# Seven block products in place of eight in two output-and-gate stages, and latent attention in nine stretches

## The chip, the cores and the metric

The kernel runs on 1 core of a Trainium2 chip. The time is device microseconds of one execution of the whole program. Before the change three runs took 4273.81, 4282.54 and 4290.16 us, median 4282.54.

TensorE multiplies (PE; PEld is its weight load), VectorE is DVE, ScalarE is ACT, GpSimd is POOL, SyncE (SP) issues the DMAs. Every matmul result lands in one of 8 PSUM banks of 512 columns; GpSimd cannot read them.

## The reference

Two model blocks one after the other, in float32, on 1024 tokens of width 1024 and 256 context tokens. Block one has a window attention layer and a latent attention layer; block two has a retention and stick-breaking layer and a RWKV-7 layer, each followed by a gated addition. What the change touches is, of block one, the attention of `latent_attention`, and of block two the end of each layer:

```python
def attend(qn, qr, kn, kr, v):                       # 16 heads, 1280 keys, value width 64
    s = (jnp.einsum("bqhd,bkhd->bhqk", qn, kn)       # 64 deep
         + jnp.einsum("bqhd,bkd->bhqk", qr, kr)).astype(F32) * scale   # 32 deep
    p = jax.nn.softmax(s, axis=-1).astype(v.dtype)
    return jnp.einsum("bhqk,bkhd->bqhd", p, v)

for i in range(DEPTH):                               # second block
    ...
    h = h + y                                        # y = mixed @ w_out, 1024 x 1024 by 1024 x 1024
    gate = jax.nn.sigmoid(jnp.einsum('bsd,de->bse', h, ple_gate[i]))
    h = h + gate * jnp.einsum('bsp,pd->bsd', p[i], ple_proj[i])
return rmsnorm(h, final_gain)
```

## The kernel before

All work is cut into row tiles of 128 tokens; there are 8 of them beside 2 of context. The program is a chain of stages with a barrier between them. In each stage every engine has its instructions written out by hand in one order and waits on semaphores (`wait_ge`) that other engines raise (`then_inc`). Nothing is scheduled by a planner.

*Latent attention* (`latent_attention`). The unit of work is a group: one pair of heads (8 pairs) by one pair of row tiles (4 pairs), 32 groups, four 128 x 1280 score blocks each. TensorE makes the scores of the next group in three chunks of 512, 512 and 256 keys into four banks (`scores`, L2107 and L2113). VectorE scales them out of the banks and takes the maxima (`read_scores` L2045, `maxima` L2052 and L2054). ScalarE takes the exponential (`exp` L2011). TensorE turns the result, four 128 x 128 blocks a bank, ten fills a group (`fill` L2122), ScalarE moves each fill to SBUF (`move` L2019), TensorE multiplies by the values (`values` L2134), VectorE copies the product out (`evacuate` L2060), TensorE turns it back (`turn_back` L2141), VectorE divides (`normalise` L2069). Two banks take the fills, one bank per head the outputs. The values of one head are made in two halves, so the TensorE order of a group alternates between scores, fills and values in 14 stretches.

*Output and gate* (`project_and_gate`, called as pg0 after stick-breaking and as pg1 at the end). For each row tile: turn the mixed row, multiply by the output weight (`output`, two halves of 512 columns, 8 blocks of depth each), add to x (L2757), copy x, turn it (L2823), multiply by the gate weight, sigmoid (L2692), multiply by p times its projection (L2763), add to x (L2765). The order interleaves the gate of tile i with the output of tile i + 2, in a loop of six rounds. pg1 also finishes the last row of the RWKV scan (class `LastOutput`; its four passes on GpSimd run from 3995.17 to 4004.34 us), norms each row tile (`norm`, L2707 to L2711 on ScalarE, L2770 on VectorE) and stores it.

*The class `Seven`* stands in the kernel already and serves the latent gate stage (`latent_gate_and_project`). It multiplies two row tiles by a 1024 x 1024 weight as a 2 x 2 block product with seven block multiplications in place of eight. The left operands are sums of blocks s1 to s4, made by GpSimd; the right ones are differences of weight blocks t1 to t4, made by VectorE once per weight; VectorE joins the products (p15, u2, c12, c22, c21). A float32 matmul in the program is two instructions in the trace, so that a block product (4 in depth) shows as x8.

Of the kernel before, what the change touches and what calls it, by code (L numbers as in the profile page):

```python
# [13 lines left out]
P = 128  # L14
# [1135 lines left out]
class Seven:  # L1150


    def __init__(self, nc, mem, name, banks):
# [3 lines left out]
        self.s1, self.s2, self.s3, self.s4 = (sb(f"s{n}", [P, HK, P]) for n in range(1, 5))  # L1157
# [784 lines left out]
def latent_attention(nc, core, q_dram, qr_dram, k_dram, kr_dram, v_dram, o, pair0, prefetch):  # L1942
# [9 lines left out]
    HALVES = [range(0, KT // 2), range(KT // 2, KT)]  # L1952
    unit = lambda h, i: 2 * h + i
    with ExitStack() as mem:
# [7 lines left out]
        pT_moved = [nc.alloc_semaphore(f"{name}_pT_moved{n}") for n in range(2)]  # L1962
# [4 lines left out]
        s_banks, pT_banks, o_banks = [core.banks(n) for n in range(4)], [core.banks(4 + n) for n in range(2)], [core.banks(6 + n) for n in range(2)]  # L1967
# [9 lines left out]
        with nc.Block() as block:  # L1977
# [28 lines left out]
            def _(act):  # L2006
# [7 lines left out]
                def move(g, f):  # L2014
# [4 lines left out]
                    act.activation(pT[:, h, at * BANK:(at + 1) * BANK], pT_banks[f % 2], ACT.Copy).then_inc(pT_moved[f % 2], 1)  # L2019
# [3 lines left out]
                for g in range(G):  # L2023
# [15 lines left out]
            def _(dve):  # L2039
# [32 lines left out]
                for g in range(-1, G + 1):  # L2072
                    if g >= 1:
                        evacuate(g - 1, 0)
                    if g + 1 < G:
                        for j in (0, 2, 1, 3):
                            read_scores(g + 1, 0, j)
                    if g >= 1:
                        normalise(g - 1, 0)
# [3 lines left out]
                    if g >= 1:  # L2083
                        evacuate(g - 1, 1)
# [5 lines left out]
                    if g >= 1:  # L2090
                        normalise(g - 1, 1)

            @block.tensor
            def _(pe):
# [21 lines left out]
                def fill(g, f):  # L2116
                    pe.wait_ge(p_made, 4 * g + (BLOCKS * f + BLOCKS - 1) // KT + 1)
                    if FILLS * g + f >= 2:
                        pe.wait_ge(pT_moved[f % 2], (FILLS * g + f) // 2)
                    for n in range(BLOCKS):  # L2120
                        j, t = (BLOCKS * f + n) // KT, (BLOCKS * f + n) % KT
                        last = pe.transpose(pT_banks[f % 2][:, n * P:(n + 1) * P], s_sb[:, g % 2, j, t * P:(t + 1) * P], core.ident)  # L2122
                    last.then_inc(pT_made, 1)

                def values(g, h, half):
                    if half == 0:
                        for n in range(2):
                            pe.wait_ge(pT_moved[n], (FILLS * g + (h + 1) * FILLS // 2 + 1 - n) // 2)
                        if g:
                            pe.wait_ge(back_read, 2 * (g - 1) + h + 1)  # L2130
# [1827 lines left out]
```

## Time and profile before

The profiled execution took 4284.42 us, its span 4282.6 us, with a mean granted TensorE clock of 0.978. TensorE is busy 4032.9 us (94%), VectorE 1540.1 (36%), ScalarE 1260.7 (29%), GpSimd 408.2 (10%). The DMA queues are busy 16.9% of the time.

| stage | from (us) | to (us) | TensorE busy in a stretch of it |
|---|---|---|---|
| latent attention | 1166 | 1758 | 562.31 of 564 us (1186 to 1750) |
| latent gate (seven products) | 1761 | 1965 | 193.05 of 194 us (1766 to 1960) |
| output and gate, pg0 | 2605 | 2887 | 225.83 of 232 us (2645 to 2877) |
| output and gate, pg1 | 3989 | 4283 | 193.79 of 195 us (4030 to 4225) |

How to read it: an instruction's line is given as L and the line of the kernel, then the engine, the operation, what is written and read, and the count where equal ones are merged. "Idle before" is the time in which the engine waited, and who ended it. Matmuls overlap, so that the time between the starts of two runs is the cost of the first, not its printed length.

### The profile page before, as it was taken

Reading aid. Unit: us, or ns where it says so; the run is one execution under the profiler, and the core shown is the slowest. Engines: PE = TensorE matmul, PEld = TensorE weight load, DVE = VectorE, ACT = ScalarE, POOL = GpSimd, SP = SyncE. Lnnn points to the kernel's source line nnn. Section 1 sums busy time; section 2 is a strip of 40 time slices with the busy share of each in tenths; the row PEclk is TensorE's granted clock in tenths of the full one; section 3 lists DMA queues with packets and bytes.
Section 4 is the critical chain, followed back from the end, with each engine's and each line's share of the span. In section 5 each row is a group of like instructions: output and inputs, shape, how many; then the busy total and the mean of one; then the engine's idle time right before and its main releaser. Section 6 shows DMA issues by size and latency. Waiting matters only on the chain. (4 is left out here: it accounts for less than half of the span.)

```text
span 4282.6 us, 70536 instructions
## 1 busy us (share of the span) xinstructions
PE 4032.9 (94%) x30002; PEld 2372.6 (55%) x30002; DVE 1540.1 (36%) x3355; ACT 1260.7 (29%) x2212; POOL 408.2 (10%) x203
## 2 busy tenths in 40 slices
PE   8999999999899999999999999989999978888998
PEld 3458844445466666544554465444444478787543
DVE  3346621132144444422331063113322356656111
ACT  1147710012255555311220063112222222211233
POOL 0000000000000000331000000000000046655100
PEclk9999999999999999999999999999999999999999
DMA  5000052141410100202012011014111221112200
GB/s 216 20 20 2 2 177 74 35 105 73 154 49 23 46 23 24 89 20 89 15 39 73 12 40 60 0 39 168 49 49 49 84 75 47 62 57 76 101 20 20
DMA packets 166054, 254.28 MB, mean 59 GB/s; under 512 B 49812, under 2 KB 95364, under 8 KB 165766
## 3 DMA queue, kind: packets, MB, share of 16 engines
q1 hardware_dynamic: 165768, 250.09, 16.9%
q8 instruction: 225, 3.69, 0.4%
q14 instruction: 61, 0.50, 0.0%
HBM read 187.76 MB, written 62.05 MB: 58 GB/s over the span
## 5 line engine op out<-in xcount | busy, mean ns | idle before, releaser
L2045 DVE TENSOR_SCALAR_CACHE_REDUCE la_s<-psum 128x512 f32<-128x512 f32 (+1 forms) x384 | 210.5, 598 | 289.7 <-PE psum L2113 289.6
L2019 ACT ACTIVATE la_pT<-psum 128x512 f32<-128x512 f32 x320 | 177.1, 596 | 236.9 <-PE psum L2122 236.9
L286 PE MATMUL psum<-room,pg_oT 128*128 128x512 f32 x512 | 229.0, 606 | 6.5 <-ACT pg_oT L2685 6.5
L286 PE MATMUL psum<-rp_w_last,rp_mixed 128*128 128x512 f32 x512 | 222.2, 592 | 0.0
L2122 PE MATMUL psum<-ident,la_s 128*128 128x128 f32 x1280 | 180.4, 280 | 2.0 <-ACT la_pT L2019 1.9
L2011 ACT ACTIVATE la_s<-la_s,la_negm 128x1280 f32<-128x1280 f32 x128 | 175.2, 1368 | 14.0 <-DVE la_negm L2054 14.0
L1167 POOL TENSOR_TENSOR lg_seven_s<-other_columns 128x512 f32<-128x512 f32 x4 | 5.1, 1267 | 1780.7 <-POOLq L112 1760.2
L286 PE MATMUL psum<-room,columns 128*128 128x512 f32 x400 | 173.3, 592 | 0.0
L286 PEld LDWEIGHTS psum<-room,pg_oT 128*128 128x128 f32 x512 | 99.3, 195 | 131.8 <-issue 127.6
L286 PE MATMUL psum<-room,rp_mixed 128*128 128x512 f32 x384 | 168.2, 594 | 3.0 <-DVE rp_mixed L3087 3.0
L3271 POOL TENSOR_TENSOR room<-room,first_weights 128x1024 f32<-128x1024 f32 x7 | 16.5, 2364 | 1603.6 <-DMA rs_b<-rwkv_raw 1535.1
L2122 PEld LDWEIGHTS psum<-ident,la_s 128*128 128x128 f32 x1280 | 137.9, 140 | 49.0 <-issue 45.3
L286 PEld LDWEIGHTS psum<-rp_w_last,rp_mixed 128*128 128x128 f32 x512 | 96.7, 190 | 119.2 <-issue 118.4
L3713 PE MATMUL psum<-rs_inverse,rs_Z 64*64 64x64 f32 x2560 | 158.5, 224 | 2.1 <-issue 0.8
L3711 PE MATMUL psum<-rs_Z,rs_inverse 64*64 64x64 f32 x2048 | 137.3, 226 | 19.8 <-DVE rs_Z L3566 19.4
L3051 ACT ACTIVATE x_rows<-psum 128x1024 f32<-128x1024 f32 x48 | 49.2, 1024 | 362.8 <-PE psum L286 362.5
L286 PE MATMUL psum<-first_weights,columns 128*128 128x512 f32 x288 | 134.0, 620 | 15.3 <-PEq L112 15.3
L2134 PE MATMUL psum<-la_pT,la_v 128*64 128x128 f32 x2240 | 146.8, 278 | 0.6 <-issue 0.6
L2107 PE MATMUL psum<-la_kT,la_qT 64*128 64x512 f32 (+1 forms) x672 | 143.1, 544 | 0.0
L286 PE MATMUL psum<-window_gate_wo,wg_ogT 128*128 128x512 f32 x320 | 141.4, 600 | 0.5 <-DVE wg_y_gated L1052 0.5
L3713 PEld LDWEIGHTS psum<-rs_inverse,rs_Z 64*64 64x64 f32 x2560 | 137.9, 140 | 3.1 <-issue 3.0
L3711 PEld LDWEIGHTS psum<-rs_Z,rs_inverse 64*64 64x64 f32 x2048 | 118.8, 141 | 23.2 <-issue 18.3
(553 smaller groups left out, 7470.6 us busy)
## 6 DMA issues: line engine op xcount, KB each, us to landing
rwkv_raw<-x_rows SPq DMA_DIRECT2D x48, 512.0 KB, 2.6
later_slots<-in_ada_w_dram SPq DMA_DIRECT2D x16, 1024.0 KB
room<-rwkv_raw SPq DMA_DIRECT2D x32, 512.0 KB, 4.6
room<-in_even_w_in_dram SPq DMA_DIRECT2D x6, 2048.0 KB, 11.3
ada_slots<-in_ada_w_dram SPq DMA_DIRECT2D x4, 2048.0 KB, 13.0
rp_w_last<-in_odd_w_in_dram SPq DMA_DIRECT2D x2, 4096.0 KB, 23.9
room<-in_odd_w_in_dram SPq DMA_DIRECT2D x3, 2048.0 KB, 12.2
latent_v<-lp_v SPq DMA_DIRECT2D x10, 512.0 KB, 2.7
```

The lines of the kernel that those rows point to most:

```text
L286: last = pe.matmul(out[:, c:c + w], left[:, k, :], right[:, k, c:c + w], start=(k == 0), stop=(k == kd - 1))
L1167: pool.tensor_tensor(self.s1[:, :, :], b[:, 0:HK, :], b[:, HK:, :], ALU.add).then_inc(self.s1_made, 1)
L2011: act.activation(s_sb[:, g % 2, j, :], s_sb[:, g % 2, j, :], ACT.Exp, bias=negm[:, g % 2, j:j + 1], accum_out=total[:, g % 2, j:j + 1]).th ...
L2019: act.activation(pT[:, h, at * BANK:(at + 1) * BANK], pT_banks[f % 2], ACT.Copy).then_inc(pT_moved[f % 2], 1)
L2045: dve.tensor_scalar(s_sb[:, g % 2, j, cols], s_banks[j][:, 0:cols.stop - cols.start], SCALE, NEG, ALU.mult, ALU.max, accum_out=smax[:, g % ...
L2107: pe.matmul(s_banks[unit(h, i)][:, 0:width], q_of[rows, queries(i)], k_of[rows, cols], start=True, stop=False)
L2122: last = pe.transpose(pT_banks[f % 2][:, n * P:(n + 1) * P], s_sb[:, g % 2, j, t * P:(t + 1) * P], core.ident)
L2134: last = pe.matmul(o_banks[h][i * B_V:(i + 1) * B_V, 0:P], v_of[:, t, h * B_V:(h + 1) * B_V], pT[:, h, i * K + t * P:i * K + (t + 1) * P], ...
L3051: act.activation(rows[:, m % 2, :], out_banks[m % 2], {G: ACT.Silu, W: ACT.Sigmoid, A: ACT.Sigmoid}.get(n, ACT.Copy)).then_inc(moved, 1)
L3271: eng.tensor_tensor(kk, k[s], k_k, ALU.mult).then_inc(q["kk_made"], 1)
L3711: pe.matmul(bank[chunk(c), n * C:(n + 1) * C], TT[chunk(c), h, :], Z[chunk(c), h, :], start=True, stop=True)
L3713: last = pe.matmul(bank[chunk(c), (GH + n) * C:(GH + n + 1) * C], Z[chunk(c), h, :], TT[chunk(c), h, :], start=True, stop=True)
```

## The change

Three things change.

1. `project_and_gate` is written anew. It works on pairs of row tiles with the class `Seven`: first the outputs of all four pairs (j = 0 to 3), then the gates of all four pairs (j = 4 to 7). The next pair's rows are turned (`turn`) between the products of this one. The sums into x are made by GpSimd (`plus`), but for the first block of an output (`c11`, VectorE). The p product is made one bank at a time (`gate`) between the block products of the gate phase. No loops are left in it. The loads of the p rows wait for two turned tiles, since p takes the room of tiles that have been turned.
2. In latent attention three banks take the fills, the two heads' outputs share the eighth bank, a head's values are made in one run, and the turn-backs and fills are grouped so that TensorE has nine stretches in a group. VectorE and ScalarE have their orders changed to match.
3. `Seven` can be given room for its sums; `LastOutput` keeps its three rows in one tensor, which the last stage reuses. The final gain and the squares go to rooms that are free by then.

The core of the diff:

```diff
@@ class Seven
-    def __init__(self, nc, mem, name, banks):
+    def __init__(self, nc, mem, name, banks, places=()):
@@ latent_attention
-        s_banks, pT_banks, o_banks = [core.banks(n) for n in range(4)], [core.banks(4 + n) for n in range(2)], [core.banks(6 + n) for n in range(2)]
+        s_banks, pT_banks, o_banks = [core.banks(n) for n in range(4)], [core.banks(4 + n) for n in range(TURNS)], [core.banks(7)[:, n * 2 * P:(n + 1) * 2 * P] for n in range(2)]
@@ ScalarE
                     exp(g, 2)
-                    move(g, 2)
-                    move(g, 3)
+                    for n in range(2, 5):
+                        move(g, n)
                     exp(g, 3)
-                    for f in range(4, 9):
-                        move(g, f)
+                    for n in range(5, 8):
+                        move(g, n)
                     if g + 1 < G:
                         exp(g + 1, 0)
+                    move(g, 8)
                     move(g, 9)
@@ VectorE
                     if g >= 1:
                         evacuate(g - 1, 0)
+                        normalise(g - 1, 0)
                     if g + 1 < G:
                         for j in (0, 2, 1, 3):
                             read_scores(g + 1, 0, j)
                     if g >= 1:
-                        normalise(g - 1, 0)
+                        evacuate(g - 1, 1)
+                        normalise(g - 1, 1)
...
@@ TensorE
-                def values(g, h, half):
...
+                def values(g, h):
+                    for n in range(TURNS):
+                        pe.wait_ge(pT_moved[n], (FILLS * g + (h + 1) * FILLS // 2 + TURNS - 1 - n) // TURNS)
+                    if 2 * g + h:
+                        pe.wait_ge(back_read, 2 * g + h)
...
                     if behind:
-                        values(g - 1, 1, 0)
+                        values(g - 1, 1)
                     if here:
                         fill(g, 2)
                         fill(g, 3)
+                        fill(g, 4)
+                    if behind:
+                        turn_back(g - 1, 1)
                     if ahead:
                         scores(g + 1, 1)
                     if here:
-                        fill(g, 4)
-                    if behind:
-                        values(g - 1, 1, 1)
-                    if here:
                         fill(g, 5)
                         fill(g, 6)
+                        values(g, 0)
                     if ahead:
                         scores(g + 1, 2)
-                    if behind:
-                        turn_back(g - 1, 1)
                     if here:
-                        values(g, 0, 0)
                         fill(g, 7)
                         fill(g, 8)
-                        values(g, 0, 1)
                         fill(g, 9)
@@ project_and_gate, TensorE
-                with pe.Fori(0, X_TILES - 2) as i:
-                    transpose_rest(i)
-                    gate(i)
-                    output(i + 2)
-                    transpose_x(i + 1)
...
+                def turn(j, n):
+                    q, i = j - PAIRS, 2 * (j % PAIRS) + n
+                    if q >= 0:
+                        pe.wait_ge(x22_made if n else x12_made, q + 1)
+                        pe.wait_ge(x21_made if n else seven.c11_read, q + 1)
...
+                    if j:
+                        pe.wait_ge(turned_read, 2 * j + n)
...
+                for j in range(J):
...
+                    seven.pe_5(pe, j, t1)
...
+                    seven.pe_6(pe, j, t2)
+                    if j + 1 < J:
+                        turn(j + 1, 0)
+                    seven.pe_3(pe, j, b22)
+                    if q >= 0:
+                        gate(4 * q + 1)
+                    if j + 1 < J:
+                        turn(j + 1, 1)
...
+                    seven.pe_7(pe, j, t3)
+                    if q >= 0:
+                        gate(4 * q + 2)
+                    if 1 <= j < 1 + X_TILES // PB:
+                        turn_p(j - 1)
+                    if j + 1 < J:
+                        begin(j + 1)
...
+                    seven.pe_4(pe, j, pair_set(j)[1], t4)
+                    if q >= 0:
+                        gate(4 * q + 3)
+                    if j + 1 < J:
+                        seven.pe_2(pe, j + 1, pair_set(j + 1)[0], weights_of(j + 1)[1])
+                    if 0 <= q + 1 < PAIRS:
+                        gate(4 * (q + 1))
@@ project_and_gate, GpSimd
+                first_sums(0)
+                last_sum(0)
                 if last is not None:
-                    last.pool_finish(pool, rest[:, X_TILES - 3, :])
+                    last.pool_finish(pool, o_row(X_TILES - 1))
@@ project_and_gate, ScalarE
+                for n in range(2):
+                    move(0, n)
                 if last is not None:
                     last.act_means(act)
+                    last.act_squares(act)
+                seven.act_p1(act, 0)
                 if last is not None:
                     last.act_norm(act)
+                    act.wait_ge(last.y_done, 1)
+                for j in range(J):
+                    q = j - PAIRS
+                    if j + 1 < J:
+                        move(j + 1, 0)
+                    if q >= 0:
+                        sig(seven.c12_read, q, g12, sig12_made)
...
+                    if q >= 0:
+                        sig(seven.c21_read, q, g21, sig21_made)
+                        if final is not None:
+                            norm_a(q)
+                    if 0 <= q + 1 < PAIRS:
+                        sig11(q + 1)
+                    if q >= 0 and final is not None:
+                        norm_b(q)
```

Three places of the order of instructions follow. First TensorE in latent attention, from the fills that follow the first 512 keys of a score to the fill before the next group's scores. `la_s` are the scores, `la_pT` the turned ones, `la_oT` an output to be turned back; `first_weights` and `columns` hold the keys and queries of the first head pair. Before:

```order
L2122 MATMUL psum<-ident,la_s 128x128 x4
L2134 MATMUL psum<-la_pT,first_weights 64x128 x10
L2122 MATMUL psum<-ident,la_s 128x128 x8
L2107 MATMUL psum<-first_weights,columns 128x256 x4
L2113 MATMUL psum<-first_weights,other_columns 128x256 x4
L2141 MATMUL psum<-ident,la_oT 128x128
L2134 MATMUL psum<-la_pT,first_weights 64x128 x10
L2122 MATMUL psum<-ident,la_s 128x128 x8
L2134 MATMUL psum<-la_pT,first_weights 64x128 x10
L2122 MATMUL psum<-ident,la_s 128x128 x4
```

After:

```order
L2140 MATMUL psum<-ident,la_oT 128x128
L2107 MATMUL psum<-first_weights,columns 128x512 x4
L2113 MATMUL psum<-first_weights,other_columns 128x512 x4
L2123 MATMUL psum<-ident,la_s 128x128 x8
L2134 MATMUL psum<-la_pT,first_weights 64x128 x20
L2107 MATMUL psum<-first_weights,columns 128x256 x4
L2113 MATMUL psum<-first_weights,other_columns 128x256 x4
L2123 MATMUL psum<-ident,la_s 128x128 x12
```

The value products stand in one run of 20 program matmuls (40 instructions) ahead of the last score chunk, the turn-back has gone up to the run before the scores, and only 12 transposes are left between the last chunk and the next group.

Next TensorE in pg0. `room2` and `room3` are the output weight's halves, `first_weights` and `room1` the gate weight's. Before, one round of the loop:

```order
L2810 MATMUL psum<-ident,pg0_o_row 128x128 x8
L286 MATMUL psum<-first_weights,pg0_xT 128x512 x8
L286 MATMUL psum<-room1,pg0_xT 128x512 x8
L286 MATMUL psum<-output0_wp,pg0_pT 128x512 x4
L2814 REGISTER_ALU
L286 MATMUL psum<-room2,pg0_oT 128x512 x8
L286 MATMUL psum<-room3,pg0_oT 128x512 x8
L2821 REGISTER_ALU
L2823 MATMUL psum<-ident,pg0_x_row 128x128 x8
```

After, a pair of the gate phase:

```order
L1188 MATMUL psum<-room1,pg0_seven_s1 128x512 x4
L1188 MATMUL psum<-pg0_t2,pg0_seven_s2 128x512 x4
L2912 MATMUL psum<-ident,x_rows 128x128 x8
L1188 MATMUL psum<-room1,pg0_seven_s4 128x512 x4
L2937 MATMUL psum<-output0_wp,even_o 128x512 x2
L2912 MATMUL psum<-ident,x_rows 128x128 x8
L1188 MATMUL psum<-pg0_t3,pg0_seven_s3 128x512 x4
L2937 MATMUL psum<-output0_wp,even_o 128x512 x2
L1188 MATMUL psum<-first_weights,x_rows 128x512 x4
L1188 MATMUL psum<-pg0_t4,pg0_other_pair 128x512 x4
L2937 MATMUL psum<-output0_wp,even_o 128x512 x2
L1188 MATMUL psum<-first_weights,x_rows 128x512 x4
```

Seven rows of four stand for two row tiles, where a tile had two rows of eight for each weight. In the output phase the rows are the same without those of L2937.

Last ScalarE at the end of pg1: `pg1_stat` is the row norm's statistics, `pg1_g12` to `pg1_g21` the blocks to be gated. Before:

```order
L2689 ACTIVATE pg1_pT<-pg1_pT_all 128x256
L2692 ACT_TABLE_LOAD
L2692 ACTIVATE pg1_sig<-psum 128x1024
L2707 ACTIVATE last_squares,pg1_stat<-x_rows 128x1024
L2709 ACT_TABLE_LOAD
L2709 ACTIVATE pg1_stat<-pg1_stat,eps 128x1
L2711 ACT_TABLE_LOAD
L2711 ACTIVATE pg1_stat<-pg1_stat 128x1
```

After:

```order
L2740 ACTIVATE pg1_g21<-pg1_g21 128x512
L2755 ACTIVATE odd_rest,pg1_stat<-x_rows 128x1024
L2757 ACT_TABLE_LOAD
L2757 ACTIVATE pg1_stat<-pg1_stat,eps 128x1
L2759 ACT_TABLE_LOAD
L2759 ACTIVATE pg1_stat<-pg1_stat 128x1
L2755 ACTIVATE odd_rest,pg1_stat<-x_rows 128x1024
L2757 ACT_TABLE_LOAD
L2757 ACTIVATE pg1_stat<-pg1_stat,eps 128x1
L2759 ACT_TABLE_LOAD
L2759 ACTIVATE pg1_stat<-pg1_stat 128x1
```

Two row norms now stand behind the last sigmoid, where one stood.

## Rows read from the trace of the kernel before

**Rows 1.** Busy time in two stretches: us, then each engine's (instructions), clock, DMA.
```profile
1186.00:1750.00 564.00, 562.31 (x5246) 364.16 (x5244) 257.28 (x1045) 331.31 (x559) 0.00 (x0) 1.00 0.10 30
1766.00:1960.00 194.00, 193.05 (x504) 89.43 (x503) 61.48 (x57) 26.77 (x41) 80.98 (x57) 1.00 0.15 52
```

**Rows 2.** TensorE in time, latent attention: start, length, instructions, idle before.
```profile
1486.36 1.99 PE L2107 MATMUL psum<-la_kT,la_qT 64*128 64x512 f32 x8
...
1490.48 1.31 PE L2134 MATMUL psum<-la_pT,la_v 128*64 128x128 f32 x20
1491.73 1.09 PE L2122 MATMUL psum<-ident,la_s 128*128 128x128 f32 x8
1492.75 1.99 PE L2107 MATMUL psum<-la_kT,la_qT 64*128 64x512 f32 x8
...
1495.74 0.66 PE L2122 MATMUL psum<-ident,la_s 128*128 128x128 f32 x4
1496.33 1.31 PE L2134 MATMUL psum<-la_pT,la_v 128*64 128x128 f32 x20
...
1500.30 0.33 PE L2141 MATMUL psum<-ident,la_oT 128*128 128x128 f32 x1
1500.56 1.31 PE L2134 MATMUL psum<-la_pT,la_v 128*64 128x128 f32 x20
...
1504.65 1.99 PE L2107 MATMUL psum<-la_kT,la_qT 64*128 64x512 f32 x8
...
1755.39 2.40 PE L2134 MATMUL psum<-la_pT,la_v 128*64 128x128 f32 x40 [0.60 <-issue]
```

**Rows 3.** TensorE and VectorE in time, behind a last score chunk.
```profile
1482.01 0.33 PE L2141 MATMUL psum<-ident,la_oT 128*128 128x128 f32 x1
...
1483.30 0.42 DVE L2045 TENSOR_SCALAR_CACHE_REDUCE la_s<-psum 128x256 f32<-128x256 f32 x1
```

**Rows 4.** TensorE and VectorE in time, pg0: entry, two rounds, last sum.
```profile
2604.61 1.06 PE L2803 MATMUL psum<-ident,even_o 128*128 128x128 f32 x8 [2.12 <-PEq L112]
2606.89 16.93 PE L286 MATMUL psum<-room,pg_oT 128*128 128x512 f32 x32 [1.21 <-ACT pg_oT L2685]
...
2644.33 7.13 PE L286 MATMUL psum<-first_weights,pg_xT 128*128 128x512 f32 x16 [0.24 <-ACT pg_xT L2702]
...
2677.48 7.13 PE L286 MATMUL psum<-first_weights,pg_xT 128*128 128x512 f32 x16 [0.24 <-ACT pg_xT L2702]
...
2885.99 1.22 DVE L2765 TENSOR_TENSOR x_rows<-x_rows,pg_add 128x1024 f32<-128x1024 f32 x1
```

**Rows 5.** Latent gate in time: TensorE's entry and two products, GpSimd's sums.
```profile
1760.62 3.40 DVE L1426 TENSOR_TENSOR x_rows<-x_rows,first_weights 128x2048 f32<-128x2048 f32 x1 [1.71 <-PEq L112]
1760.70 3.67 PE L1188 MATMUL psum<-first_weights,columns 128*128 128x512 f32 x8 [2.18 <-PEq L112]
1761.95 3.19 POOL L1173 TENSOR_TENSOR lg_seven_s<-lg_seven_s,columns 128x512 f32<-128x512 f32 x1
...
1765.06 3.70 PE L1188 MATMUL psum<-first_weights,columns 128*128 128x512 f32 x8 [0.69 <-ACT lg_seven_p L1230]
1765.22 1.27 POOL L1179 TENSOR_TENSOR lg_seven_s<-columns,lg_seven_s 128x512 f32<-128x512 f32 x1
...
1875.09 3.60 PE L1188 MATMUL psum<-lg_wo,lg_seven_s 128*128 128x512 f32 x8
...
1899.12 1.91 PE L1485 MATMUL psum<-ident,latent_o 128*128 128x128 f32 x16
```

**Rows 6.** pg1 in time: VectorE's and TensorE's entry, the last norm.
```profile
3989.43 1.23 DVE L3191 TENSOR_REDUCE last_mean<-psum 128x16 f32<-128x1024 f32 x1 [5.83 <-PEq L112]
...
3991.96 15.60 PE L286 MATMUL psum<-room,pg_oT 128*128 128x512 f32 x32 [1.47 <-ACT pg_oT L2685]
...
4272.80 1.06 ACT L2707 ACTIVATE last_squares<-x_rows 128x1024 f32<-128x1024 f32 x1 [4.99 <-DVE x_rows L2765]
...
4277.10 1.28 DVE L2770 SCALAR_TENSOR_TENSOR x_rows<-x_rows,pg_stat,pg_gain 128x1024 f32<-128x1024 f32 x1 [4.34 <-ACT pg_stat L2711]
```

More of the change, by code:

```diff
@@ L2623, in _, with project_and_gate @@
                 outputs(LAST)
-def project_and_gate(nc, core, a, name, layer, heads, rest, weights, rows=None, heads_in=None, last=None, final=None, following=None):
+def project_and_gate(nc, core, a, name, layer, o_row, weights, other, places, t4, p_rows, pT_all, rows=None, heads_in=None, last=None, final=None, following=None):
     PD = 2
-    PB = BANK // (PD * P)
+    PB = 2 * BANK // (PD * P)
+    PAIRS = X_TILES // 2
+    J = 2 * PAIRS
     with ExitStack() as mem:
@@ L2645, in project_and_gate @@
+        pp_bank = lambda m: core.banks(6 + m % 2)
+        top, low = (lambda w: w[:, 0:HK, :]), (lambda w: w[:, HK:, :])
+        weights_of = lambda j: (top(wo0), low(wo0), low(wo1), top(wo1)) if j < PAIRS else (top(wg0), low(wg0), low(wg1), top(wg1))
+        blocks = lambda t: t.rearrange("p (k t) -> p k t", k=KD)
         if final is not None:
-            gain, stat, squares = sb("gain", [P, D]), sb("stat", [P, 2]), last.squares
+            gain, stat = final[2], sb("stat", [P, 2])
+            squares = final[3]
@@ new lines, in sums @@
+                def sums(j):
+                    seven.dve_p15(dve, j)
+                    if j == 0:
+                        t_3(0)
+                    seven.dve_u2(dve, j)
+                    if j == 0:
+                        if last is not None:
+                            dve.wait_ge(last.y_done, 1)
+                        t_4(0)
+                    if j == PAIRS - 1:
+                        t_2(PAIRS)
+                for n in ("wo0", "wo1"):
+                    dve.wait_ge(weights.arrived[n], 16)
@@ new lines, in turn_p @@
+                def turn_p(n):
+                    if n == 0:
+                        pe.wait_ge(p_in, 16)
+                        if last is not None:
+                            pe.wait_ge(last.dev_made, 1)
+                    else:
+                        pe.wait_ge(p_moved, n)
+                    for t in range(PB):
+                        for k in range(PD):
+                            at = (t * PD + k) * P
+                            end = pe.transpose(p_banks[:, at:at + P], p_rows[:, n * PB + t, k * P:(k + 1) * P], core.ident)
+                    end.then_inc(p_turned, 1)
@@ new lines, in gate @@
+                def gate(m):
+                    q, at = m // 4, m % 4
+                    i, half = 2 * q + at // 2, (0, 1, 1, 0)[at]
+                    if m >= 2:
+                        pe.wait_ge((out11_made, out12_made, out22_made, out21_made)[(m - 2) % 4], (m - 2) // 4 + 1)
+                    else:
+                        pe.wait_ge(p_moved, X_TILES // PB)
+                        pe.wait_ge(weights.arrived["wp"], 16)
+                    for k in range(PD):
+                        end = pe.matmul(pp_bank(m), pT_all[:, i, k * P:(k + 1) * P], wp[:, k, half * BANK:(half + 1) * BANK], start=k == 0, stop=k == PD - 1)
+                    end.then_inc(pp_made, 1)
```

393 lines of the change are left out of this document (209 added, 184 removed).

## The prediction

> **What bounds the kernel now.** I read the page's engine line first (TensorE busy 94% of the span, told with the table above), then the busy time by stage, then TensorE's instructions in order of time inside the three stages that the diff touches. In the attention stage TensorE is busy 562.3 of 564.0 us, clock 1.00 [rows 1]; no engine is waited for, so a us taken from its stream is a us of the span, as long as VectorE and ScalarE keep up. Both output-and-gate stages run at a fixed 33.15 us per row tile (2644.33 to 2677.48) [rows 4]. The stage between them that already multiplies by seven block products, the latent gate, has TensorE busy 193.1 of 194.0 us at clock 1.00 [rows 1]: that is my template.
>
> **Attention, what is removed.** A stretch is a run of matmuls of one kind. The reader is to see in [rows 2] that a stretch costs its matmuls and something more. Four transposes last from 1495.74 to 1496.33, 0.59 us; eight last from 1491.73 to 1492.75, 1.02. So one transpose is 0.11 us and the stretch itself 0.155. The 20 value matmuls take 1.25 us (1490.48 to 1491.73); the run of 40 at the stage's end lasts 2.40 where one of 20 lasts 1.31, so a value matmul is 0.055 us, and again 0.155 is over. The 32 groups (8 head pairs by 4 tile pairs) go from 14 stretches to nine: two value stretches and three transpose stretches go (the turn-back, 0.26 us alone at 1500.30, joins the run before scores). Five times 0.155 is 0.77 us, 32 times 24.5 us. A group now takes 18.29 us (1486.36 to 1504.65).
>
> **Attention, what it adds.** After the last score chunk of a group came 4.35 us of other work before the next scores; now come only 12 transposes, 1.46 us. Those scores write the banks that VectorE is still emptying. In [rows 3] the stretch behind the 256-wide chunk starts at 1482.01, and VectorE's third read of that chunk (the other head's bank, after the maxima of the first) starts at 1483.30 and takes 0.42: 1483.72. TensorE would be ready at 1483.47. The first scores thus stand 0.25 us plus a semaphore step, 0.30, 32 times 9.6 us. Queued behind them on TensorE is everything of the next group. From below this can be nothing (if the read's end counts earlier); from above 0.6, if the weight loads start cold and the fourth read is waited for. I take 0.30. The other new orders I laid out along the same group: VectorE's normalise now stands before its score reads and waits for the turn-back (0.33 us long); since both heads' outputs share a bank, the value products wait for the other head's normalise, which ends 0.45 us before the second head's and 3.7 us before the first head's are due; the value products find their moves done by more than 2 us; a third transpose bank only relaxes ScalarE, busy under 60%. Net for the stage: 24.5 less 9.6 less a start and an end that gain nothing, 14 us. Ends: 24 and 3.
>
> **Output and gate, products.** Per pair of tiles and weight, eight block products become seven. One product is eight instructions; the template's seven take 24.03 us from 1875.09 to 1899.12, 3.43 each [rows 5]. A stage has 4 pairs by 2 weights, so 8 products or 27.5 us go in each stage. The rest of TensorE's work is the same: 16 row turns of 8 transposes (0.87 each), 16 transposes of p, 64 instructions for the p product (0.43 each).
>
> **Output and gate, waits.** The other gain is that outputs come first for all pairs and gates after: the sum that a gate needs is done a whole phase before. The new stage 0 is the sum: 2.28 us to the first product, as before (2604.61 to 2606.89, the second turn lies inside it) [rows 4]; the first two products with the copy of P1 between them 7.8 (1760.70 to 1765.06, and 3.43) [rows 5]; 54 products 185.4; 14 turns 12.2; p 1.7; p product 27.5: 236.9. The clock was granted low after the stage's entry: its first 32 instructions took 16.93 for some 13.9 [rows 4], so 3.4 us more with the rest: 240.3. Behind the last p product come a multiply on VectorE (0.7) and a sum on GpSimd (1.3): 242.4. Before it was 2604.61 to 2887.21, 282.6 us (2885.99 and 1.22). Gain 40 us, of it 27.5 in products and 12.7 in stalls.
>
> Stage 1 has the same TensorE work. Its first products also ran slow (15.60) [rows 6]; I put 3.4 there too. ScalarE's second move waits until GpSimd has finished the last scan row: four passes, 9.2 us (3995.17 to 4004.34, told above), which now stand behind the first four block sums. I get y done some 21 to 24 us in, and the turn behind it due at 23: 0.5 us. TensorE ends after 240.8 us. The tail is longer: VectorE's last sum, the sigmoid and then two row norms one after the other, each 4.30 us on ScalarE (4272.80 to 4277.10) and 1.28 on VectorE [rows 6], where before only one was left. From the end of the last block product: 0.75, 0.65, 5.6, 5.6, with the p product's 1.7 beside it. 240.8 less 1.7 plus 12.7 is 251.8. Before: 3989.43 to 4278.38, 289.0. Gain 37 us, 3 less for that tail.
>
> The weight differences (t1 to t4, 2.8 to 3.4 us each on VectorE) and the block sums (GpSimd) I cost at nothing: the template does the same with TensorE never waiting after its start. The cover is the 24 to 33 us of TensorE's pair against 4 block sums and 3 or 4 row sums of 1.27, some 10 us on GpSimd, and on VectorE under 12. If it were gone, a pair would wait at its first sum product. The norms on ScalarE (two per pair, 8.6 us, and table loads) fit too: the last ends some 12 us after a pair's last product, the next turn is due at 14.6. This is the tightest place of the gate phase in stage 1.
>
> **A rule against it.** In [rows 5] a GpSimd sum beside VectorE's weight difference took 3.19 us, the next one 1.27. The Trainium skill, page "SBUF — State Buffer", section "SBUF: two separate sides", says that the two share a port pair as an exclusive lock and that the loser blocks for the whole instruction; the trace agrees (3.19 against 1.27). It makes the Pool chain a rival, priced below.
>
> **The sum.** 14, 40 and 37 make 91 us off the profiled execution's 4284.4 us (span 4282.6): 4193.4. That execution is 1.9 us above the median 4282.5, so I say 4192 us.
>
> **Rivals.**
> 1. *No stall in attention.* The removed stretches pay in full (24 us) and the slow clock after the entries is not granted low again (6 us): 4192 less 10 less 6, 4176. For it: 0.25 us is a small overlap, read from one group. Against: TensorE cannot be released before VectorE's read. 14%.
> 2. *Attention gives little.* A stall of 0.6 us per group leaves 3 to 5 us: 4202. For: a wait at the head of a stretch also holds its weight load. 14%.
> 3. *GpSimd's chain comes onto the path* in the output-and-gate stages. Eight weight differences per stage, each blocking one sum by 1.9 us; with stage 1's y finish behind them: up to 16 times 1.9, 30 us: 4222. Against: in the template, with the same eight differences, TensorE's idle time is 0.9 us in all from 1766 to 1960 [rows 1]. 6%.
> 4. *The nine-stretch attention loses the clock*, the one that ends slower. The granted clock is at 1.00 from 1186 to 1750 [rows 1] with TensorE never idle; now there would be an idle moment in every group, before a longer run of transposes. At half clock a stretch takes twice as long, so what decides is how long a group runs low: the 91 us of gain over 32 groups are 2.84 us, reached when 5.7 of a group's 17.8 us run at half clock. With 7 of 17.8 it would be 3.5 us a group, 112 us, 4304. Against: the idle moment is 0.3 us, and the template passed 0.69 us with no loss. 2%. The Trainium skill, page "TensorE: Matmul & The Clock Gate", section "Part 4: PE-mode transpose", says that transposes don't count as busy for the clock gate in the same way; the trace of before, 40 transposes a group at clock 1.00, doesn't bear it out.
> 5. *The change does not do what it says.* The order of instructions shows seven rows of four block matmuls per pair and the nine stretches, so I leave it 1%.
>
> **Chances.** The forecast, within its own bounds of 4182 to 4200, holds 63%; the rivals 14, 14, 6, 2 and 1%. The range that holds 8 in 10 takes in rivals 1 and 2 and part of 3: 4174 to 4212. About 0.5% (21 us) is what a measurement of this kernel can tell from no change; every case but 4 and 5 is beyond it: faster 0.97, same 0.01, slower 0.02.
>
> **What would show it.** Right: a group of 17.8 us with a wait of about 0.3 for VectorE's score read at the head of the first scores, transposes in runs of 8, 13 and 12, value runs of 40; stage 0 at 242 us from first turn to last sum, in which 56 block products of 3.43 are 192; clock 1.00 outside the first 30 us. Stage 1 at 252 us with two norms after TensorE's end. Wrong: a group above 18.1 us, a group at clock under 1.00, or TensorE waiting for GpSimd's block sums inside a phase.

## The result, and the profile after

The changed kernel took 4182.22 us, median of 4 runs (4176.67 to 4183.86); the kernel before, beside it on the same chip, 4286.35 (4273.81 to 4293.55). The ratio is 0.9764, 95% interval 0.9746 to 0.9782: by the ratio, faster by 101 us, 93 to 109. The profiled execution took 4180.71 us with a span of 4178.9, 103.7 less than the span before.

The table cuts both spans at the same marks on TensorE, each the start of a stage's first transposes or products. The text calls these the marks.

| from, to | before (us) | after (us) | difference |
|---|---|---|---|
| start of attention's fills, latent gate | 580.6 | 565.9 | -14.7 |
| latent gate, retention | 235.8 | 237.3 | +1.5 |
| retention, stick-breaking | 497.1 | 498.7 | +1.7 |
| stick-breaking, pg0 | 111.1 | 112.2 | +1.1 |
| pg0, RWKV projections | 288.9 | 245.7 | -43.1 |
| RWKV projections, scan | 546.8 | 546.6 | -0.2 |
| scan, pg1 | 549.2 | 539.0 | -10.2 |
| pg1, TensorE's end | 280.8 | 238.6 | -42.2 |
| behind TensorE's end | 12.4 | 14.9 | +2.5 |

Busy time by stretch, after: attention, the latent gate, pg0, the scan and pg1. The columns are those of [rows 1]: stretch, its length, busy time (instructions) of PE, PEld, DVE, ACT and POOL, clock, DMA.

```profile
1186.00:1720.00 534.00, 526.17 (x5089) 355.12 (x5088) 248.91 (x1020) 322.78 (x540) 0.00 (x0) 1.00 0.10 31
1753.00:1947.00 194.00, 193.05 (x505) 89.37 (x504) 59.84 (x57) 26.67 (x41) 79.31 (x56) 1.00 0.13 49
2594.12:2839.84 245.72, 236.22 (x657) 112.05 (x657) 61.76 (x72) 38.31 (x49) 82.58 (x60) 0.99 0.13 43
3386.41:3924.18 537.77, 467.96 (x13627) 438.68 (x13627) 342.98 (x536) 105.55 (x167) 309.83 (x135) 0.97 0.18 58
3925.45:4164.01 238.56, 236.41 (x656) 111.97 (x656) 72.18 (x76) 68.41 (x90) 95.69 (x63) 1.00 0.14 53
```

and of the kernel before, pg0, the scan and pg1 between the same marks:

```profile
2604.61:2893.47 288.86, 270.51 (x721) 126.53 (x721) 30.46 (x28) 47.14 (x57) 0.00 (x0) 0.98 0.11 37
3440.24:3988.16 547.92, 472.61 (x13626) 444.50 (x13626) 344.44 (x536) 105.79 (x167) 310.18 (x135) 0.96 0.17 57
3989.43:4270.18 280.75, 270.97 (x720) 126.60 (x720) 39.55 (x32) 82.42 (x104) 8.94 (x4) 0.98 0.12 47
```

Attention is no longer full: 7.8 of 534 us idle, where [rows 1] had 1.7 of 564. Pg0 has exactly 64 instructions fewer, the eight products. Its TensorE time falls by 34.3 us and its idle time from 18.4 to 9.5 (8.6 of which stand in front of the next stage's first transposes). GpSimd now works 82.6 us in pg0 and 95.7 in pg1. TensorE waits for it once, 1.03 us at the entry of pg1.

One attention group of the changed kernel, the answer to [rows 2] and [rows 3] (start, length, instructions, idle before): VectorE's reads of the last chunk, and TensorE.

```profile
1459.55 0.08 DVE L2047 DVE_READ_ACCUMULATOR la_s<-psum 128x1 f32 x1
1459.74 0.16 DVE L2054 TENSOR_REDUCE la_top<-la_smax 128x2 f32<-128x6 f32 x1
1459.93 0.17 DVE L2056 TENSOR_SCALAR la_negm<-la_top 128x2 f32<-128x2 f32 x1
1460.01 0.42 DVE L2047 TENSOR_SCALAR_CACHE_REDUCE la_s<-psum 128x256 f32<-128x256 f32 x1
...
1460.49 1.99 PE L2107 MATMUL psum<-la_kT,la_qT 64*128 64x512 f32 x8 [0.24 <-DVE la_s L2047]
...
1464.61 2.40 PE L2134 MATMUL psum<-la_pT,la_v 128*64 128x128 f32 x40
1466.94 1.53 PE L2123 MATMUL psum<-ident,la_s 128*128 128x128 f32 x12
1468.31 0.27 PE L2140 MATMUL psum<-ident,la_oT 128*128 128x128 f32 x1
...
1478.34 0.70 PE L2107 MATMUL psum<-la_kT,la_qT 64*128 64x512 f32 x2 [0.24 <-DVE la_s L2047]
```

A group takes 17.85 us (1460.49 to 1478.34). TensorE is ready 0.24 us too early, and starts when VectorE's third read, begun at 1460.01 behind the maxima of the first head, has ended.

Pg0's entry, the answer to [rows 4] and [rows 5], TensorE and GpSimd in time:

```profile
2594.12 1.94 PE L2912 MATMUL psum<-ident,even_o 128*128 128x128 f32 x16 [2.13 <-PEq L112]
2596.29 3.70 PE L1188 MATMUL psum<-room,pg_other_pair 128*128 128x512 f32 x8 [0.24 <-ACT pg_other_pair L2725]
2597.23 2.70 POOL L1167 TENSOR_TENSOR pg_seven_s<-pg_other_pair 128x512 f32<-128x512 f32 x1 [644.92 <-ACT pg_other_pair L2725]
2600.01 1.27 POOL L1173 TENSOR_TENSOR pg_seven_s<-pg_seven_s,pg_other_pair 128x512 f32<-128x512 f32 x1
2600.68 3.70 PE L1188 MATMUL psum<-room,pg_other_pair 128*128 128x512 f32 x8 [0.69 <-ACT pg_seven_p L1230]
2604.22 3.60 PE L1188 MATMUL psum<-room,pg_seven_s 128*128 128x512 f32 x8
2607.65 3.60 PE L1188 MATMUL psum<-pg_t,pg_seven_s 128*128 128x512 f32 x8
```

The products follow each other 3.43 us apart from the third on (2604.22, 2607.65). The first eight-instruction product takes 3.70 at full clock, where [rows 4] had 16.93 for 32, that is 4.2 for eight.

Pg1's one stall, the answer to the entry in [rows 6]: GpSimd's passes over the last scan row, VectorE's weight difference beside one of them, ScalarE's move, TensorE.

```profile
3935.65 1.90 POOL L3337 TENSOR_TENSOR last_rows<-last_rows,last_var 128x1024 f32<-128x1024 f32 x1
3937.62 2.35 POOL L3339 TENSOR_TENSOR last_rows<-last_rows 128x1024 f32<-128x1024 f32 x1
3939.99 2.28 DVE L2810 TENSOR_TENSOR pg_t<-pg_t,room 128x2048 f32<-128x2048 f32 x1
3940.05 4.44 POOL L3341 TENSOR_TENSOR last_rows<-last_rows,x_rows 128x1024 f32<-128x1024 f32 x1
3944.57 2.34 POOL L3343 TENSOR_TENSOR odd_rest<-last_rows,x_rows 128x1024 f32<-128x1024 f32 x1
3946.95 1.02 ACT L2725 ACTIVATE x_rows<-psum 128x1024 f32<-128x1024 f32 x1 [11.90 <-POOL odd_rest L3343]
3948.12 1.06 PE L2912 MATMUL psum<-ident,odd_rest 128*128 128x128 f32 x8 [1.03 <-ACT x_rows L2725]
```

y, the finished last scan row, is done 21.5 us in (3925.45 to 3946.9). ScalarE then moves it, and TensorE's turn (the transposes of that row), for which TensorE was ready 21.6 us in, stands 1.03 us.

### The profile page after: what moved, and what is told of

Read it like the earlier page. It is cut to its first block and busy times, and to the rows that moved or that the text cites. A ratio compares the mean times of both kernels' runs of the same rounds, so it can differ in the third digit from the quotient of the medians.

```text
span 4178.9 us, 70398 instructions
## 1 busy us (share of the span) xinstructions
PE 3940.7 (94%) x29874; PEld 2340.7 (56%) x29874; DVE 1599.6 (38%) x3443; ACT 1244.1 (30%) x2195; POOL 577.9 (14%) x323
## 5 line engine op out<-in xcount | busy, mean ns | idle before, releaser
L2011 ACT ACTIVATE la_s<-la_s,la_negm 128x1280 f32<-128x1280 f32 x128 | 174.6, 1364 | 17.8 <-DVE la_negm L2056 14.0
L2123 PE MATMUL psum<-ident,la_s 128*128 128x128 f32 x1280 | 166.2, 277 | 0.1
L2134 PE MATMUL psum<-la_pT,la_v 128*64 128x128 f32 x2240 | 134.6, 275 | 0.7 <-ACT la_pT L2020 0.7
L3819 PE MATMUL psum<-rs_inverse,rs_A 64*64 64x64 f32 x2560 | 106.0, 221 | 25.7 <-DVE rs_inverse L3681 25.3
L286 PEld LDWEIGHTS psum<-room,columns 128*128 128x128 f32 x400 | 76.0, 190 | 95.7 <-issue 95.7
L835 DVE CUSTOM_DVE_ANT_0 wa_s<-psum,window_mask_rows 128x640 f32<-128x640 f32 (+1 forms) x128 | 100.6, 786 | 71.1 <-PE psum L890 71.1
L2134 PEld LDWEIGHTS psum<-la_pT,la_v 128*64 128x64 f32 x2240 | 121.2, 137 | 10.1 <-issue 9.0
## 6 DMA issues: line engine op xcount, KB each, us to landing
ada_slots<-in_ada_w_dram SPq DMA_DIRECT2D x4, 2048.0 KB, 13.7
room<-in_odd_w_in_dram SPq DMA_DIRECT2D x3, 2048.0 KB, 12.5
```

The costliest lines, as they stand in the source:

```text
L286: last = pe.matmul(out[:, c:c + w], left[:, k, :], right[:, k, c:c + w], start=(k == 0), stop=(k == kd - 1))
L835: dve.tensor_tensor_reduce(out=s_sb[:, u % 2, b, 0:n], in0=s_banks[b][:, 0:n], in1=mask[:, lo:lo + n], scale=1.0, scalar=NEG, op0=ALU.add, ...
L2011: act.activation(s_sb[:, g % 2, j, :], s_sb[:, g % 2, j, :], ACT.Exp, bias=negm[:, g % 2, j:j + 1], accum_out=total[:, g % 2, j:j + 1]).th ...
L2123: last = pe.transpose(pT_banks[turn][:, n * P:(n + 1) * P], s_sb[:, g % 2, j, t * P:(t + 1) * P], core.ident)
L2134: last = pe.matmul(o_banks[h][i * B_V:(i + 1) * B_V, 0:P], v_of[:, t, h * B_V:(h + 1) * B_V], pT[:, h, i * K + t * P:i * K + (t + 1) * P], ...
L3819: last = pe.matmul(core.banks(2 + m % 2)[chunk(c), n * C:(n + 1) * C], A[chunk(c), 0, h, 0, :], T[chunk(c), h, :], start=True, stop=True)
```

## The experiments

Eight kernels, in two sets; the kernel before took 4277.82 us beside the first four and 4280.11 beside the others. Every ratio is to the kernel before of the same set.

**E1, the new attention alone**, in the kernel before.

```diff
 # class latent_attention as after, everything else as before
-    HALVES = [range(0, KT // 2), range(KT // 2, KT)]
+    TURNS = 3
```

> The kernel before with the new latent attention alone. Theory A (five stretches of 0.155 us less per group, a wait of 0.3 us more, 32 groups): the stage loses 15 us, a group lasts 17.85 us against 18.29, and the program is 15 us shorter, ratio 0.9966; the RWKV scan of this program takes what it takes in the kernel before, 534 us from its last projection to the last scan row give or take 10 us of granted clock. Theory B (the 10 us that the scan lost in the changed kernel belong to the change of the output stages, its rooms and its unrolled code): the scan stays at the length of before, within 2 us, here and in the unchanged kernel. Rival: the new stretch order gains only beside the other change: ratio above 0.999.

4263.02 us, ratio 0.9967 (0.9954 to 0.9979): 14 us. Attention takes 565.9 us between the marks, as in the changed kernel.

**E2, the new output-and-gate stages alone**, with the old attention.

```diff
 # project_and_gate, Seven and LastOutput as after
-    TURNS = 3
+    HALVES = [range(0, KT // 2), range(KT // 2, KT)]
```

> The changed kernel with the latent attention of before. Theory A: the two output-and-gate stages give 43 and 39.5 us as in the changed kernel, together 82, and the program is 80 to 93 us shorter than before depending on what clock the scan is granted, ratio 0.979 to 0.981. The attention group is back at 18.29 us. Theory B: the scan is 10 us shorter here as in the changed kernel and the whole is 92 us shorter, ratio 0.9785.

4194.92 us, ratio 0.9797 (0.9774 to 0.9819): 87 us. Pg0 245.7 and pg1 239.8 us (pg1 here and below is counted from the start of the scan's last product to TensorE's end; the changed kernel has 239.8 too). The two ratios multiplied are 0.9765, and the whole change has 0.9764: the two parts add up, within what these times can tell.

**E3, all reads of the last score chunk before the maxima.**

```diff
                         for h in range(2):
                             for i in range(2):
                                 read_scores(g + 1, 2, unit(h, i))
+                        for h in range(2):
                             maxima(g + 1, h)
```

> The changed kernel; VectorE reads all four score banks of the last chunk before it takes the two maxima, so that the third bank is free 0.37 us earlier. Theory A (the idle time at the head of each group is the wait for that third read): the wait of 0.24 to 0.33 us per group goes, a group lasts 17.55 us against 17.85, the program is 9 us shorter than the changed kernel. Rival C (the idle time is the fourth read, or the cold start of the stretch after transposes): 3 us or less. Rival D: the exponential, started 0.7 us later, becomes late for the first fill and the group is longer than 17.85 us.

4170.88 us, ratio 0.9749 (0.9729 to 0.9769), some 6 us below the changed kernel's 0.9764, with intervals that overlap. The reading rests on the stage: attention falls from 565.9 to 556.5 us. It repeats well, 565.8 to 565.9 in the four profiles of the changed order (the changed kernel, E1, E5, E6) and 556.5 and 556.6 in the two with the reads first (E3, E7). TensorE in a stretch of it, of E3:

```profile
1186.00:1710.00 524.00, 524.00 (x5085) 354.08 (x5084) 243.37 (x1018) 319.70 (x540) 0.00 (x0) 1.00 0.11 32
```

It is busy 524.00 of 524.00 us. Two reads, a few tenths earlier, take the whole wait away, with the stretches untouched. 9.4 us by 32 groups are 0.29 us each, what the stall cost. Without it attention is 24.1 us shorter than before (580.6 to 556.5), what the prediction gave the five stretches (24.5).

**E4, each head's values in two runs again**, so 13 stretches in place of nine (the other head's run is split in the same way).

```diff
-                        fill(g, 6)
-                        values(g, 0)
+                        values(g, 0, 0)
+                        fill(g, 6)
+                        values(g, 0, 1)
```

> The changed kernel with each head's value products cut into two runs again by a fill moved between them: four stretches more in a group, 13 in place of nine, every instruction the same. Theory A (0.155 us per stretch): a group lasts 17.85 + 0.62 = 18.47 us and the program is 20 us longer than the changed kernel. Rival E (the gain came from the third transpose bank and the later moves, not from the number of stretches): under 5 us longer.

4203.62 us, ratio 0.9815 (0.9790 to 0.9840). Attention takes 585.0 us, 19.1 more than with nine stretches: 4 stretches by 32 groups are 128, so a stretch costs 0.15 us. The instructions, the three banks and the wait at the head of the group are those of the changed kernel, so neither the third bank nor the later moves made this gain. Of E4 in time, values and fills again in short runs, and the wait still at the head of the scores:

```profile
1463.27 1.31 PE L2135 MATMUL psum<-la_pT,la_v 128*64 128x128 f32 x20
1464.51 0.66 PE L2124 MATMUL psum<-ident,la_s 128*128 128x128 f32 x4
1465.10 1.31 PE L2135 MATMUL psum<-la_pT,la_v 128*64 128x128 f32 x20
...
1469.82 1.99 PE L2108 MATMUL psum<-la_kT,la_qT 64*128 64x512 f32 x8 [0.24 <-DVE la_s L2048]
```

**E5, an eighth product again, in the new order.**

```diff
+        if self.twice:
+            for k in range(HK):
+                pe.matmul(self.x[j % 2], a[:, k, :], b11[:, k, :], ...)
         self.pe_sum(pe, self.x[j % 2], a[:, 0:HK, :], b11, True, self.made1)
```

> The changed kernel with the first block product of each pair and weight made twice, in both output-and-gate stages: eight products of eight instructions for seven (its result is overwritten by the same values). 16 more products of 3.43 us are 54.9 us. Theory P (a product costs its length, since TensorE waits for nobody in these stages): 4182 + 55 = 4237 us against the changed kernel, 0.989 of the kernel before; stage pg0 from 245.7 to 273.2 us and stage pg1 from 239.8 to 267.3 us between the same two marks on TensorE, and what is left of their gain over the kernel before (43 and 40 us) is 15 and 12 us, the stalls. Rival W (the seven are bound by the engines behind them, so that an extra product hides): under 40 us in all, below 4222.

4238.55 us, ratio 0.9902 (0.9875 to 0.9928), for 4237 and 0.989 expected. Pg0 is 273.2 us for 245.7, +27.5; pg1 265.8 for 239.8, +26.1, a little less since the longer first products cover pg1's stall for y. TensorE's count is that of the old kernel, and pg0 is still 15.7 us shorter than before (288.9). Pg0 of E5:

```profile
2592.88:2866.06 273.18, 263.68 (x720) 124.40 (x721) 61.72 (x72) 38.32 (x49) 82.53 (x60) 0.99 0.12 39
```

Beside the kernel before, idle time is 9.5 for 18.4 us (8.9 less) and busy time 6.8 less at the same count. Of these 6.8, some 4.6 are the clock (an estimate: in the old pg0 TensorE was busy 9.2 us at half clock, in the new one not at all); what the other 2.2 are is open.

**E6, the last norms earlier in pg1's last pair.**

```diff
+                    if final is not None and q == PAIRS - 1:
+                        norm_a(q)            # ScalarE: behind the sigmoid of c12
...
+                    if early:
+                        norm(2 * q - 1)      # VectorE: in front of c22
...
+                    if early:
+                        norm(2 * q)          # VectorE: behind c22, in front of its gate
```

> The changed kernel with the end of stage pg1 in another order: the second-to-last row norm is made as soon as its row is ready, in front of the last sigmoid's sum on VectorE and behind it on ScalarE, and not after the last tile's sum. In the trace of the changed kernel the last block product ends at 4162.33 and the last sum at 4174.87, 12.5 us. If the two norms one after the other set this tail (my reading), it becomes 9 to 10 us, 3 us less in all: 4179, ratio to the kernel before some 0.0007 lower, which only the trace can tell. Rival: the last tile's own chain (sum, sigmoid, sum, squares, norm) sets it and nothing changes.

4178.55 us, ratio 0.9764 (0.9741 to 0.9787): by the times, nothing that can be told. In the trace the part from the last p product's start to the last sum's end is 10.69 us for 12.74, so 2.05 less, not 3. ScalarE and VectorE in time at the end of E6:

```profile
4162.78 1.28 ACT L2740 ACT_TABLE_LOAD   x1
4162.80 1.28 DVE L2834 SCALAR_TENSOR_TENSOR x_rows<-x_rows,pg_stat,odd_rest 128x1024 f32<-128x1024 f32 x1 [3.28 <-ACT pg_stat L2759]
4163.72 1.88 PE L2944 MATMUL psum<-first_weights,odd_rest 128*128 128x512 f32 x4
4164.07 0.63 ACT L2740 ACTIVATE pg_g<-pg_g 128x512 f32<-128x512 f32 x1
4164.73 0.69 DVE L2830 TENSOR_TENSOR pg_g<-pg_g,psum 128x512 f32<-128x512 f32 x1 [0.66 <-ACT pg_g L2740]
4165.34 0.68 DVE L1257 TENSOR_TENSOR pg_g<-psum,pg_seven_p 128x512 f32<-128x512 f32 x1
```

The norm now stands between two sigmoids and costs ScalarE one more table load (ACT_TABLE_LOAD, 1.28 us), so the sigmoid of c22 is late. VectorE's last join (L1257) stands behind the product that needs this sigmoid (L2830), and starts 1.62 us after the p product's start, where it started 0.20 after it. So some 3.5 us would have been won, and 1.4 of them were given back.

**E7, three edits together**: E3, E6, and this in pg1.

```diff
-                last_sum(0)
                 if last is not None:
                     last.pool_finish(pool, o_row(X_TILES - 1))
+                last_sum(0)
...
-                t_2(0)
                 if last is not None:
                     last.dve_variances(dve)
+                t_2(0)
```

> The changed kernel with three edits: VectorE reads all four banks of a group's last score chunk before it takes maxima (9 to 11 us less, as measured alone); the end of stage pg1 as in the run before (3 us less); and at the start of stage pg1 GpSimd finishes the last scan row before its first block sum, so that y is done earlier (1.2 us less, the stall behind x_rows). Sum 14 to 15 us below the changed kernel: 4168, 0.973 of the kernel before. If the early finish only moves the wait to the first pair's block sums, the third part turns into a loss of up to 5 us, and the whole is worth 8 to 10.

4165.40 us (4161.28 to 4170.01), ratio 0.9732 (0.9710 to 0.9755), below the changed kernel's by 0.0032 or 14 us; the best of all. The intervals touch, but the slowest of these five runs is 6 us under the fastest of the changed kernel's four. By the marks it is 9.3 in attention, 0.8 in pg1 up to TensorE's end and 2.0 behind it, 12 in all. The third edit gives 0.8 where 1.2 was expected. GpSimd, VectorE, ScalarE and TensorE of E7 show why:

```profile
3920.43 2.28 DVE L2807 TENSOR_TENSOR pg_t<-room 128x2048 f32<-128x2048 f32 x1
3921.18 3.29 POOL L3345 TENSOR_TENSOR last_rows<-last_rows,last_var 128x1024 f32<-128x1024 f32 x1 [1.06 <-ACT last_var L3340]
...
3926.97 2.35 POOL L3349 TENSOR_TENSOR last_rows<-last_rows,x_rows 128x1024 f32<-128x1024 f32 x1
3927.58 3.89 DVE L2813 TENSOR_TENSOR pg_t<-pg_t,room 128x2048 f32<-128x2048 f32 x1
3929.40 4.28 POOL L3351 TENSOR_TENSOR odd_rest<-last_rows,x_rows 128x1024 f32<-128x1024 f32 x1
...
3934.88 1.06 PE L2920 MATMUL psum<-ident,odd_rest 128*128 128x128 f32 x8 [0.21 <-ACT x_rows L2726]
```

Two of the four passes now start while a weight difference (L2807, L2813) stands on VectorE: 12.3 us in all (3.29, 2.34, 2.35, 4.28) for 11.0 in the changed kernel. y is done 20.6 us in, for 21.5, and TensorE waits 0.21 us for 1.03.

**E8, the kernel before again**, for a second profile.

> The kernel before once more, for a second profile. In the comparison the scan stage, which the change does not touch, was 10 us shorter after than before (547.9 to 537.8 us from its first decay sum to its last). Theory A (the scan's length varies from execution to execution, by where the low granted clock falls and how waits line up, and the first profile of the kernel before was a long one): this profile has a scan of 532 to 545 us, with the same code; the run with the old output-and-gate stages and the new attention had 533.6. Theory B (the scan gains by the change): it is again within 2 us of 547.9.

4283.49 us, ratio 1.0007 (0.9991 to 1.0023). The scan of E8, and below it that of E1, which also has the old stages behind the scan:

```profile
3436.57:3977.31 540.74, 472.34 (x13627) 443.57 (x13626) 340.79 (x536) 105.63 (x167) 309.18 (x135) 0.95 0.17 58
```

```profile
3429.29:3962.91 533.62, 467.90 (x13626) 438.92 (x13626) 339.70 (x536) 105.56 (x167) 310.76 (x135) 0.96 0.17 58
```

Three profiles with the old stages have 547.9, 540.7 and 533.6 us. Seven with the new ones have 534.0 to 544.6. Theory B falls: by E8 and E1 the scan's 10 us is no more than what one execution of the old stages differs from another. Why they differ is not settled: TensorE's half-clock time in the scan was 47.8, 51.2 and 41.0 us in the three, and E2 had 47.8 with 538.7 us, so the clock alone doesn't order them. Most of the 14.3 us between the first profile and E1 is idle time of TensorE (75.3 for 65.7 us).

E8 also shows the old pg1 with an entry at full clock, where [rows 6] had a slow one:

```profile
3981.11 13.97 PE L286 MATMUL psum<-room,pg_oT 128*128 128x512 f32 x32 [1.47 <-ACT pg_oT L2685]
```

## Why the prediction was right

Predicted was 4192, within 4182 to 4200, and measured 4182, at the lower edge. By its steps:

- **Attention, 14 us less: right, with both of its terms.** 14.7 by the marks, 14 by E1. The stretch at 0.155 us is borne out by E4 (0.15), the wait of 0.30 by E3 (0.29, of which the trace shows 0.24 as idle). A group of 17.85 us for 17.8, values in 2.40, fills of 12 in 1.53. Of rival 1 one half (no stall) fell by the trace and became E3's edit; the other half, no slow clock after the entries, came true. Rival 2 needed a stall of 0.6 us.
- **Eight products fewer in each stage, 27.5 us: right**, measured by E5 as 27.5 in pg0 and 26.1 in pg1. Where two products follow each other without a wait, one is 3.43 us, as in the latent gate.
- **The rest of pg0, 12.7 us: 15.7 measured.** TensorE's part from the first turn to the last p product's end is 237.1 us (2594.12 to 2831.26), where the sum without the clock's 3.4 was 236.9. The term that was wrong is those 3.4 us. I put the slow entry of [rows 4] in again because the entry looked the same; the clock was not granted low there. 242.4 us to the last sum were forecast, 239.3 came (2594.12 to 2833.40). The forecast called its 12.7 stalls; by E5 the 15.7 are 8.9 of waiting and 6.8 of busy time, most of that the clock.
- **Pg1, 37 us: 39.5 from first transpose to last sum** (289.0 to 249.4). Again the 3.4 us of clock were not there. The stall for y was 1.03 us and not 0.5. Y came 21.5 us in, inside the 21 to 24 that I gave it, but TensorE was ready for the turn 21.6 us in and not 23. On y's side, GpSimd's third pass, beside VectorE's weight difference, took 4.44 us, where it took 2.34 in the kernel before and 2.35 in E7; this cost I had weighed as a rival and left out of the chain to y, and without its 2.1 us y would have been in time (an estimate). The tail was 12.5 us for 12.7. (The prediction's terms add up to 12.6 here, and to 242.3 for pg0 and not 242.4.) The 3.4 us were also read from one execution: of the three profiles of the old pg1, E8's has no slow entry (13.97 us for the 32 instructions that took 15.60 in [rows 6]). From pg1's first transposes to the end of the span the three take 290.7 (E8), 293.2 and 293.9 us (E1), the changed kernel 253.5, so the gain is 37 to 40 us by which of them is called before.
- **Nothing elsewhere: by chance about right.** The stages between attention and pg0 took 4.2 us more, with 47.7 us at half clock for 37.5 before; the scan 10.2 less. The scan's part is no effect of the change that can be told (E8). Of the 4.2 us, 2.8 are in retention and stick-breaking, which are as long as in the changed kernel in E2, with the old attention (498.6 and 112.2 us), and as short as before in E4 and E5, with the new one (497.0 and 111.0, 497.1 and 111.0). The 1.5 us in the latent gate may well belong to the change, against this step: six of the seven profiles with the new attention have a half-clock period of 3.4 us at its entry and 237.0 to 237.8 us there, and the three with the old one have none and 235.6 to 235.8. E3 is the seventh, with the new attention, no such period and 235.6 us. What brings the period on is open.
- **Rival 3, GpSimd's chain** (up to 30 us): GpSimd's long passes came (4.44 and 2.70 us above), but no product inside a phase waits; only the entry of pg1 does, and E7 moves that wait. The Trainium skill's page "SBUF — State Buffer", section "SBUF: two separate sides", says that the one that comes second waits for the whole instruction of the other; the trace agrees, 4.44 being 2.35 and nearly the 2.28 of the weight difference.
- **Rival 4, the clock in attention**: 1.00 in the whole stretch with the wait in every group. The transposes stand between score and value products in every group, so no run here shows what clock transposes alone would be granted.

The forecast for the profiled execution was 4193.4 us and it took 4180.7, 12.7 less. By the marks 0.7 of this is in attention, 3.1 in pg0 and 2.7 in pg1, mostly the two clock terms (3.4 each, with small misses the other way), and 6.1 are the stages that the change was to leave alone, the scan above all. So about half of the miss is the forecast's own, and about half lies outside the three stages and is mostly chance.

## What to carry to other kernels

Where TensorE's stream is full, count its stretches, the runs of matmuls of one kind: each has a price that can be measured (here 0.15 us, five times in each of 32 groups). Then look at what the moved work used to cover. Here 9.4 of 24.5 us were lost again to a read of the scores that stood behind maxima, and one line that put the reads before the maxima won them back. Lay out the start and the end of a stage operation by operation, with the table loads and with the waits between VectorE and GpSimd, since both edits there gave two thirds of what their simple sum promised. And do not carry a slow clock from one profile into a forecast for a new order: it was the largest wrong term in both stages.

## What the runs showed of the hardware that I had not expected

- **The new output-and-gate stages hold the clock.** In the seven profiles with the new pg1 no half-clock time falls into it up to TensorE's end; the three with the old have 10.2, 13.7 and 6.8 us. In pg0 up to the next stage it is 4.3 to 5.5 for 14.3 to 14.4, and the 4.3 to 5.5 lie in the idle time behind TensorE's last product. E5, with the old number of products, keeps the clock too (5.5 and 0), so it goes with the order and its fewer waits, or with the instruction mix, and not with the amount of work. Which of these it is I did not try.
- **A stage with the same code differs by 14 us.** The scan took 533.6 to 547.9 us over ten profiles (14 us are 0.3% of the span), so a profile of before and one of after can show a difference of 10 us in a stage that the change does not touch. A second profile of the old kernel showed it.
- **Contention works both ways.** In E7 VectorE's weight difference (3927.58) started inside GpSimd's third pass (3926.97 to 3929.32) and took 3.89 us, for 2.28 at the same place in the changed kernel. GpSimd's fourth pass (3929.40) started inside that difference and took 4.28 for 2.34. Each time the one that started second is the long one.
